# A border between two experts in a float32 MoE decoder kernel: weight split first, result read-out in pieces

## The chip, the cores and the metric

The kernel runs on one core of one Trainium2 chip. The metric is the device time of one launch in microseconds (us). Before the change it is 1759.11 us, the median of three runs (1756.7 to 1759.35). The profile is of one further execution, which took 1762.06 us.

The engines are called by these names: PE is TensorE (matrix multiplication; PEld is its weight load), DVE is VectorE, ACT is ScalarE, POOL is GpSimd, SP is SyncE, which issues the weight transfers.

## What is computed

The reference is one inference step of a small decoder trunk with two layers, for 256 prompt tokens and 8 sample tokens, all in float32. Layer 0 ends in a dense SwiGLU, layer 1 in a mixture of eight experts, of which every token uses two:

```python
def swiglu(x, wg, wu, wd):
    return (jax.nn.silu(x @ wg) * (x @ wu)) @ wd

def moe_swiglu(x, w_r, wg, wu, wd):
    logits = (x @ w_r).astype(jnp.float32)
    top_v, top_i = lax.top_k(logits, TOP_K)
    gates = jax.nn.softmax(top_v, axis=-1)
    ...
    for e in range(N_EXPERTS):
        out = out + dense_gate[..., e:e + 1].astype(x.dtype) * swiglu(x, wg[e], wu[e], wd[e])
    return out
```

The model width is 1024 and an expert's hidden width 3584. One expert's three weight matrices are 44 MB in float32.

## The kernel before, in words

The first 730 us (both mixers, the dense feed-forward, the router) are not touched. The change is in the expert stage, which runs from about 735 us to 1747 us.

**Jobs and units.** The expert stage consists of eight jobs, one for each expert. A job gathers up to 120 tokens of its expert and the 8 sample tokens into a block of 128 columns, multiplies, and adds the result back a job later. Its weights come in 42 units of 1 MB (128 partitions x 2048 values), in the order of the table STREAM (line 235): in each of 7 steps the gate weights g in two units, the up weights u in two, and from the second step on the down weights d of the step before, in two; the last two units are d of the last step. So a job begins with units 0, 1 (g), 2, 3 (u), 4, 5 (g), 6, 7 (u), 8, 9 (d), and ends with 40, 41 (d). Below, "unit 2" means unit 2 of the next job where a border between two jobs is spoken of.

**Splitting.** The products are done in the type float32r, so each unit is split in two parts whose sum is the float32 value: ACT copies the unit to w_hi (rounded), then DVE computes w_lo = unit - w_hi, and PE multiplies three times: high by high, low by high, high by low. A unit is 12 matmuls with 512 columns. There are three buffers for w_hi and three for w_lo (SPLITS = 3): the split of unit p needs PE to be through with unit p-3. The raw units lie in a ring of six (RING), which SP refills when DVE has written the w_lo of the unit six before.

**Queues.** Each engine has its own program, written out by hand in order: `job(...)` for PE at line 1348, for ACT at line 1693, for DVE at line 2278. An engine does its instructions in that order, and semaphores make one wait for another. In ACT's and DVE's programs the loop variable p runs from 3 to 44; at p the unit p is split (for p of 42 to 44 units 0 to 2 of the next job, `split(j, p)`), and the other work that goes with unit p-3 follows. PE, in its order, does the two g units, then (from step 1) the transposes of the step before, then the two u units, then down.

**Other work in a step.** When the g product is done, ACT writes silu of it (act_g, in act_place). When the u product is done, DVE multiplies it with act_g to act_h (line 2290, also in act_place). PE transposes act_h (line 1298, the operation with ident), ACT and DVE split the transpose into at_hi and at_lo, and PE multiplies that with the down weights into two banks of PSUM (Y_BANKS).

**The border.** Behind the last matmul of unit 41 the result of the job lies in the two Y banks. ACT reads each half to ysb_hi, scaled with the gate (`high_result`, line 1689). DVE's `results` (line 2256) does four operations: for each half ysb_lo = scaled bank - ysb_hi for all 128 rows, then for rows 96 to 127 (the sample tokens) acc = scaled bank + acc (shown as moe_rows). The last of them raises y_free, which PE awaits at step 1 before it writes the Y banks again. ysb_hi and ysb_lo are used by PE from step 1 of the next job (`scatter`, one quarter in each of four steps). On both engines the read-out stands ahead of `split(j, 44)`, the split of unit 2 of the next job.

ACT, DVE and PE run jobs 0 to 6 in a hardware loop and job 7 in code written out behind it. There are seven borders between jobs.

Of the kernel before, what the change touches and what calls it, by code (L numbers as in the profile page):

```python
# [23 lines left out]
F32 = mybir.dt.float32  # L24
F32R = mybir.dt.float32r
I32 = mybir.dt.int32
ALU = mybir.AluOpType
# [17 lines left out]
NE, FE = 8, 3584  # L45
# [6 lines left out]
SPLITS = 3  # L52
# [194 lines left out]
PER_JOB = len(STREAM)  # L247
# [9 lines left out]
def trunk(nc, a, o):  # L257

    with ExitStack() as ctx:
# [6 lines left out]
        bank = [ctx.enter_context(nc.psum_tensor(f"bank{i}", [P, 512], F32)) for i in range(8)]  # L266
# [165 lines left out]
        acc = carve(3, D)  # L432
# [16 lines left out]
        gslot = carve(1)  # L449
# [14 lines left out]
        ysb_hi, ysb_lo = (sb(n, [P, D], F32R) for n in ("ysb_hi", "ysb_lo"))  # L464
# [75 lines left out]
        y_free = sem("y_free")  # L540
# [859 lines left out]
        def _(act):  # L1400
# [39 lines left out]
            def split(j, p, first=False):  # L1440

                if not first:
                    used(j, p - SPLITS)
                slot = p % RING
                act.wait_ge(w_landed[slot], 16 * (landed0[slot] + j * (PER_JOB // RING) + p // RING + 1))
                f(w_hi[p % SPLITS][:, :], wring[:, slot, :]).then_inc(hi_ready, 1)
# [236 lines left out]
            def high_slots(j):  # L1683

                for i, b in enumerate(X_BANKS):
                    act.wait_ge(full[b], moe0[b] + j + 1)
                    high_part(i)
# [5 lines left out]
            def job(j, more, last=False):  # L1693


                for p in range(SPLITS, PER_JOB + SPLITS):
                    if p == PER_JOB + SPLITS - 1:
                        act.wait_ge(evac[S_BANK], moe0[S_BANK] + (j + 1) * S_FILLS)
                        if last:
                            act.wait_ge(y0_full, 1)  # L1700
                            high_result(0)
                    if p < PER_JOB:
                        split(j, p)
                    else:
                        used(j, p - SPLITS)
                    mat, s, h = STREAM[p - SPLITS]
                    n = j * STEPS + s
                    if (mat, h) == ("g", 1):
                        if s > 0:
                            act.wait_ge(full[T_BANK], moe0[T_BANK] + n)  # L1710
                            f(at_hi[:, (s - 1) % 2], bank[T_BANK][:, :]).then_inc(at_hi_ready, 1)
                        f(act_g[:, s % 2, :], bank[G_BANK][:, :], ACT.Silu).then_inc(evac[G_BANK], 1)
                    if (mat, s, h) == ("d", STEPS - 2, 1):
                        act.wait_ge(full[T_BANK], moe0[T_BANK] + n + 2)
                        f(at_hi[:, (STEPS - 1) % 2], bank[T_BANK][:, :]).then_inc(at_hi_ready, 1)
                        if not last:
                            high_slots(j)
                    if p == PER_JOB + SPLITS - 1:
                        for h in range(1 if last else 0, 2):
                            high_result(h)  # L1720
                    if p >= PER_JOB and more:
                        split(j, p)

            def last_results(n):

# [34 lines left out]
        def _(dve):  # L1760
# [21 lines left out]
            def stt(out, in0, scalar, in1, op0=ALU.mult, op1=ALU.add):  # L1782
                return V.scalar_tensor_tensor(out=out, in0=in0, scalar=scalar, in1=in1, op0=op0, op1=op1)  # L1783
# [15 lines left out]
            def split(j, p):  # L1799

                dve.wait_ge(hi_ready, j * PER_JOB + p + 1)
                tt(w_lo[p % SPLITS][:, :], wring[:, p % RING, :], w_hi[p % SPLITS][:, :].bitcast(F32), ALU.subtract
                   ).then_inc(lo_ready, 1)
# [449 lines left out]
                v = acc[:, t, 512 * h:512 * h + 512]  # L2253
                return tt(v, v, out[:, :], ALU.add)

            def results(j):

                for h in range(2):
                    dve.wait_ge(ysb_ready, 2 * j + h + 1)
                    hs = slice(512 * h, 512 * h + 512)  # L2260
                    stt(ysb_lo[:, hs], bank[Y_BANKS[h]][:, :], gslot[:, :], ysb_hi[:, hs].bitcast(F32), ALU.mult,
                        ALU.subtract).then_inc(ylo_ready, 1)
                    v = acc[ROWS[2], 2, hs]
                    ins = stt(v, bank[Y_BANKS[h]][ROWS[2], :], gslot[ROWS[2], :], v, ALU.mult, ALU.add)
                ins.then_inc(y_free, 1)

            def low_part(s, n):
                dve.wait_ge(at_hi_ready, n + 1)
# [6 lines left out]
                    dve.wait_ge(xg_hi_ready, 2 * j + 2 + i + 1)  # L2275
                    low_slots(i, bank[b]).then_inc(evac[b], 1)

            def job(j, more, last=False):

                for p in range(SPLITS, PER_JOB + SPLITS):  # L2280
                    if p < PER_JOB:
                        split(j, p)
                    mat, s, h = STREAM[p - SPLITS]
                    n = j * STEPS + s
                    if (mat, h) == ("g", 1) and s > 0:
                        low_part(s - 1, n - 1)
                    if (mat, h) == ("u", 1):
                        dve.wait_ge(evac[G_BANK], moe0[G_BANK] + n + 1)
                        dve.wait_ge(full[U_BANK], moe0[U_BANK] + n + 1)
                        tt(act_h[:, s % 2, :], act_g[:, s % 2, :], bank[U_BANK][:, :], ALU.mult  # L2290
                           ).then_inc(evac[U_BANK], 1)
                    if (mat, h) == ("d", 1) and s < 5:
                        dve.wait_ge(full[S_BANK], moe0[S_BANK] + j * S_FILLS + s + 1)
                        if s < 4:
                            add_back(bank[S_BANK], s).then_inc(evac[S_BANK], 1)
                    if (mat, s, h) == ("d", 4, 1):
                        V.tensor_copy(gslot[:, :], bank[S_BANK][:, 2 * P:2 * P + 1])
                        V.tensor_copy(sct[:, :, :], bank[S_BANK][:, 0:2 * P].rearrange("p (t n) -> p t n", t=2)
                                      ).then_inc(evac[S_BANK], 1)
                        dve.wait_ge(evac[S_BANK], moe0[S_BANK] + (j + 1) * S_FILLS)  # L2300
                        if not last:
                            choose(j + 1)
                    if (mat, s, h) == ("d", STEPS - 2, 1):
                        low_part(STEPS - 1, n + 1)
                        if not last:
                            next_low_slots(j)
                    if p == PER_JOB + SPLITS - 1:
                        results(j)
                    if p >= PER_JOB and more:
                        split(j, p)  # L2310


            for t in range(3):
# [2 lines left out]
            V.memset(sct[:, :, :].bitcast(F32), 0.0)  # L2316
            V.memset(ysb_hi[:, :].bitcast(F32), 0.0)
            V.memset(ysb_lo[:, :].bitcast(F32), 0.0).then_inc(y_free, 1)
            with dve.Fori(0, NE - 1) as j:
                job(j, True)  # L2320
            dve.wait_ge(passes_ready, 1)
            jobs = nc.values_load(passes[0:1, 0:1], engines=[DVE], min_val=NE, max_val=JOBS)
            job(NE - 1, False, last=True)
            with nc.If(jobs > NE):
                choose(NE)
                for p in range(SPLITS):
# [47 lines left out]
```

## Time and profile before

| | |
|---|---|
| Time, median of 3 runs | 1759.11 us (1756.7 to 1759.35) |
| The profiled execution | 1762.06 us |
| Its span, from the first to the last instruction | 1760.3 us |
| PE busy | 1710.1 us, 97% of the span |
| DVE busy | 1356.7 us, 77% |
| ACT busy | 1055.5 us, 60% |
| Granted TensorE clock, mean | 0.992 |
| Moved by DMA | 465.51 MB |

The span is cut from the trace of one execution. Busy shares are averages over the whole program: in the expert stage DVE and the DMA queues are far busier than in the first half. Ends of matmuls are modelled: a matmul of 512 columns is shown with about 0.39 us, but the next one starts 0.23 us after it, since they overlap. For the pace of PE the starts have to be read, not the durations. On DVE and ACT, too, an operation can start a little before the one ahead of it has ended. A wait is shown in square brackets behind the instruction that waited, with what released it.

### The profile page before, as it was taken

Reading aid. Unit: us, or ns where it says so; the run is one execution under the profiler, and the core shown is the slowest. Engines: PE = TensorE matmul, PEld = TensorE weight load, DVE = VectorE, ACT = ScalarE, POOL = GpSimd, SP = SyncE. Lnnn points to the kernel's source line nnn. Section 1 sums busy time; section 2 is a strip of 40 time slices with the busy share of each in tenths; the row PEclk is TensorE's granted clock in tenths of the full one; section 3 lists DMA queues with packets and bytes.
Section 4 is the critical chain, followed back from the end, with each engine's and each line's share of the span. In section 5 each row is a group of like instructions: output and inputs, shape, how many; then the busy total and the mean of one; then the engine's idle time right before and its main releaser. Section 6 shows DMA issues by size and latency. Waiting matters only on the chain.

```text
span 1760.3 us, 24065 instructions
## 1 busy us (share of the span) xinstructions
PE 1710.1 (97%) x8992; PEld 1440.2 (82%) x8992; DVE 1356.7 (77%) x1376; ACT 1055.5 (60%) x1013; POOL 112.3 (6%) x117
## 2 busy tenths in 40 slices
PE   7999999999999999999999999999999999999996
PEld 5877899999887789888788788788788788787885
DVE  3678766664357876688888888888888988888886
ACT  2535544433243554677777776776776766777675
POOL 2054000000105400000000000000000000000000
PEclk9999999999999999899999999999999999999999
DMA  8455354646545535499899899899899999998993
GB/s 254 144 179 180 130 173 144 187 134 180 184 132 172 189 122 190 153 362 359 316 367 354 315 363 358 322 360 351 324 358 333 346 357 322 356 360 309 368 359 111
DMA packets 257159, 465.51 MB, mean 264 GB/s; under 512 B 8492, under 2 KB 108196, under 8 KB 257056
## 3 DMA queue, kind: packets, MB, share of 16 engines
q1 hardware_dynamic: 250736, 443.28, 72.8%
q0 software_dynamic: 6064, 20.19, 3.3%
q8 instruction: 46, 0.75, 0.2%
q10 hardware_dynamic: 288, 1.08, 0.2%
q14 instruction: 25, 0.20, 0.0%
HBM read 453.70 MB, written 11.15 MB: 264 GB/s over the span
## 4 chain that ended last, share of the span: by engine, by line
PE 87%; DVE 7%; ACT 3%; issue 2%; POOL 0%; DVEq 0%; ACTq 0%; POOLq 0%
PE bank L884 84%; PE bank L888 3%; DVE arena L1783 2%; DVE w_lo L1786 1%; ACT w_hi L1414 1%; ACT arena L1414 1%; DVE moe_rows L1783 1%; DVE fw_lo L1786 1%; ACT fw_hi L1414 1%; DVE cs_t L1786 0%; DVE arena L1786 0%; DVE sam_y L1875 0%; DVE ysb_lo L1783 0%; DVE bank L1997 0%; DVE rs L1786 0%
## 5 line engine op out<-in xcount | busy, mean ns | idle before, releaser
L1786 DVE TENSOR_TENSOR w_lo<-wring,w_hi 128x2048 fp32r<-128x2048 f32 x336 | 768.4, 2291 | 109.7 <-ACT w_hi L1414 108.9
L1414 ACT ACTIVATE w_hi<-wring 128x2048 fp32r<-128x2048 f32 x336 | 644.4, 1920 | 250.4 <-PE bank L884 250.3
L884 PE MATMUL bank<-w_hi,xg_hi 128*128 128x512 f32 x896 | 357.4, 399 | 13.6 <-DVE w_lo L1786 12.1
L884 PE MATMUL bank<-w_hi,xg_lo 128*128 128x512 f32 x896 | 353.5, 395 | 0.0
L884 PE MATMUL bank<-w_lo,xg_hi 128*128 128x512 f32 x896 | 352.4, 393 | 0.0
L884 PE MATMUL bank<-hn,wring 128*128 128x264 f32 x1152 | 269.1, 391 | 8.5 <-DVE hn L1783 6.1
L884 PEld LDWEIGHTS bank<-hn,wring 128*128 128x128 f32 x1152 | 218.6, 192 | 51.5 <-issue 11.7
L884 PEld LDWEIGHTS bank<-w_hi,xg_hi 128*128 128x128 f32 x896 | 168.3, 188 | 54.7 <-DVE w_lo L1786 13.7
L884 PEld LDWEIGHTS bank<-w_lo,xg_hi 128*128 128x128 f32 x896 | 168.4, 188 | 38.1
L884 PEld LDWEIGHTS bank<-w_hi,xg_lo 128*128 128x128 f32 x896 | 168.5, 188 | 36.2
L884 PE MATMUL bank<-w_hi,at_hi 128*128 128x512 f32 x448 | 177.9, 397 | 1.8 <-DVE at_lo L1786 1.8
L1786 DVE TENSOR_TENSOR fw_lo<-wring,fw_hi 128x2048 fp32r<-128x2048 f32 (+1 forms) x54 | 113.1, 2095 | 83.7 <-ACT fw_hi L1414 83.7
L884 PE MATMUL bank<-w_lo,at_hi 128*128 128x512 f32 x448 | 176.3, 394 | 0.0
L884 PE MATMUL bank<-w_hi,at_lo 128*128 128x512 f32 x448 | 175.2, 391 | 0.0
L1414 ACT ACTIVATE fw_hi<-wring 128x2048 fp32r<-128x2048 f32 (+1 forms) x54 | 95.0, 1760 | 124.4 <-PE bank L884 124.4
L1414 ACT ACTIVATE arena<-bank 128x11 f32<-128x11 f32 (+4 forms) x96 | 31.9, 349 | 162.9 <-PE bank L884 162.9
L1783 DVE SCALAR_TENSOR_TENSOR arena<-bank,par,arena 128x255 f32<-128x255 f32 (+2 forms) x120 | 57.6, 481 | 70.8 <-ACT arena L1414 67.8
L884 PEld LDWEIGHTS bank<-w_hi,at_hi 128*128 128x128 f32 x448 | 84.1, 188 | 20.7 <-DVE at_lo L1786 2.0
L884 PEld LDWEIGHTS bank<-w_lo,at_hi 128*128 128x128 f32 x448 | 84.1, 188 | 20.2
L884 PEld LDWEIGHTS bank<-w_hi,at_lo 128*128 128x128 f32 x448 | 84.5, 189 | 19.6
L884 PE MATMUL bank<-hn_hi,fw_hi 128*128 128x264 f32 x352 | 87.6, 285 | 2.1 <-DVE xT L1786 2.1
L884 PE MATMUL bank<-hn_hi,fw_lo 128*128 128x264 f32 x352 | 87.5, 284 | 0.0
(261 smaller groups left out, 2055.4 us busy)
## 6 DMA issues: line engine op xcount, KB each, us to landing
wring<-in_moe_w_gate SPq DMA_DIRECT2D x112, 1024.0 KB, 5.7
wring<-in_moe_w_up SPq DMA_DIRECT2D x112, 1024.0 KB, 5.5
wring<-in_moe_w_down SPq DMA_DIRECT2D x112, 1024.0 KB, 5.3
wring<-in_w_in SPq DMA_DIRECT2D x36, 1024.0 KB, 5.3
wring<-in_w_out SPq DMA_DIRECT2D x16, 1024.0 KB, 5.2
wring<-in_ffn_w_gate SPq DMA_DIRECT2D x11, 1024.0 KB, 5.5
wring<-in_ffn_w_up SPq DMA_DIRECT2D x11, 1024.0 KB, 5.4
wring<-in_ffn_w_down SPq DMA_DIRECT2D x16, 704.0 KB, 4.7
```

The source lines that it names most:

```text
L884: return nc.tensor.matmul(out, lhsT, rhs, start=start, stop=stop)
L888: return nc.tensor.transpose(out, in_, ident[0:k, 0:k])
L1414: return nc.scalar.activation(out, in_, fn, **kw)
L1783: return V.scalar_tensor_tensor(out=out, in0=in0, scalar=scalar, in1=in1, op0=op0, op1=op1)
L1786: return V.tensor_tensor(out, in0, in1, op)
```

## The change

On ACT, `split(j, p)` for the last three p of a job now stands ahead of the `high_result` pair, so that at p = 44 the w_hi of unit 2 is written before ysb_hi.

On DVE, `results` is cut into `low_result` (the ysb_lo of one half) and `sample_result` (the acc rows of one half; the second raises y_free). All four are taken out of the border and put into the next job: behind the split of unit 3 stands low_result(0), behind unit 4 sample_result(0), behind unit 5 low_result(1), behind unit 6 sample_result(1), this last one ahead of act_h of step 0. Job 7 does its own four at its end, as before. Job 0 has no predecessor, so it is written out ahead of DVE's loop, which now runs jobs 1 to 6. PE's and SP's programs are unchanged.

```diff
--- before.py
+++ after.py
@@ -1715,11 +1715,11 @@
                         f(at_hi[:, (STEPS - 1) % 2], bank[T_BANK][:, :]).then_inc(at_hi_ready, 1)
                         if not last:
                             high_slots(j)
+                    if p >= PER_JOB and more:
+                        split(j, p)
                     if p == PER_JOB + SPLITS - 1:
                         for h in range(1 if last else 0, 2):
                             high_result(h)
-                    if p >= PER_JOB and more:
-                        split(j, p)
 
             def last_results(n):
 
@@ -2253,16 +2253,19 @@
                 v = acc[:, t, 512 * h:512 * h + 512]
                 return tt(v, v, out[:, :], ALU.add)
 
-            def results(j):
-
-                for h in range(2):
-                    dve.wait_ge(ysb_ready, 2 * j + h + 1)
-                    hs = slice(512 * h, 512 * h + 512)
-                    stt(ysb_lo[:, hs], bank[Y_BANKS[h]][:, :], gslot[:, :], ysb_hi[:, hs].bitcast(F32), ALU.mult,
-                        ALU.subtract).then_inc(ylo_ready, 1)
-                    v = acc[ROWS[2], 2, hs]
-                    ins = stt(v, bank[Y_BANKS[h]][ROWS[2], :], gslot[ROWS[2], :], v, ALU.mult, ALU.add)
-                ins.then_inc(y_free, 1)
+            def low_result(j, h):
+
+                dve.wait_ge(ysb_ready, 2 * j + h + 1)
+                hs = slice(512 * h, 512 * h + 512)
+                stt(ysb_lo[:, hs], bank[Y_BANKS[h]][:, :], gslot[:, :], ysb_hi[:, hs].bitcast(F32), ALU.mult,
+                    ALU.subtract).then_inc(ylo_ready, 1)
+
+            def sample_result(h):
+
+                v = acc[ROWS[2], 2, 512 * h:512 * h + 512]
+                ins = stt(v, bank[Y_BANKS[h]][ROWS[2], :], gslot[ROWS[2], :], v, ALU.mult, ALU.add)
+                if h == 1:
+                    ins.then_inc(y_free, 1)
 
             def low_part(s, n):
                 dve.wait_ge(at_hi_ready, n + 1)
@@ -2275,11 +2278,15 @@
                     dve.wait_ge(xg_hi_ready, 2 * j + 2 + i + 1)
                     low_slots(i, bank[b]).then_inc(evac[b], 1)
 
-            def job(j, more, last=False):
+            def job(j, more, results_due=False, results_later=False, last=False):
 
                 for p in range(SPLITS, PER_JOB + SPLITS):
                     if p < PER_JOB:
                         split(j, p)
+                    if results_due and p in (SPLITS, SPLITS + 2):
+                        low_result(j - 1, (p - SPLITS) // 2)
+                    if results_due and p in (SPLITS + 1, SPLITS + 3):
+                        sample_result((p - SPLITS) // 2)
                     mat, s, h = STREAM[p - SPLITS]
                     n = j * STEPS + s
                     if (mat, h) == ("g", 1) and s > 0:
@@ -2304,10 +2311,12 @@
                         low_part(STEPS - 1, n + 1)
                         if not last:
                             next_low_slots(j)
-                    if p == PER_JOB + SPLITS - 1:
-                        results(j)
                     if p >= PER_JOB and more:
                         split(j, p)
+                    if p == PER_JOB + SPLITS - 1 and not results_later:
+                        for h in range(2):
+                            low_result(j, h)
+                            sample_result(h)
 
 
             for t in range(3):
@@ -2316,11 +2325,12 @@
             V.memset(sct[:, :, :].bitcast(F32), 0.0)
             V.memset(ysb_hi[:, :].bitcast(F32), 0.0)
             V.memset(ysb_lo[:, :].bitcast(F32), 0.0).then_inc(y_free, 1)
-            with dve.Fori(0, NE - 1) as j:
-                job(j, True)
+            job(0, True, results_later=True)
+            with dve.Fori(1, NE - 1) as j:
+                job(j, True, results_due=True, results_later=True)
             dve.wait_ge(passes_ready, 1)
             jobs = nc.values_load(passes[0:1, 0:1], engines=[DVE], min_val=NE, max_val=JOBS)
-            job(NE - 1, False, last=True)
+            job(NE - 1, False, results_due=True, last=True)
             with nc.If(jobs > NE):
                 choose(NE)
                 for p in range(SPLITS):
```

DVE, the end of the loop body before (the border; w_lo here are units 0, 1 and, behind the four results, 2 of the next job):

```order
L1786 TENSOR_TENSOR w_lo<-wring,w_hi 128x2048 [waits hi_ready]
L2259 REGISTER_ALU
L1783 SCALAR_TENSOR_TENSOR ysb_lo<-bank,route,ysb_hi 128x512 [waits ysb_ready]
L1783 SCALAR_TENSOR_TENSOR moe_rows<-bank,route,moe_rows 32x512
L2259 REGISTER_ALU
L1783 SCALAR_TENSOR_TENSOR ysb_lo<-bank,route,ysb_hi 128x512 [waits ysb_ready]
L1783 SCALAR_TENSOR_TENSOR moe_rows<-bank,route,moe_rows 32x512
L1801 REGISTER_ALU
L1786 TENSOR_TENSOR w_lo<-wring,w_hi 128x2048 [waits hi_ready]
L2319 REGISTER_ALU
L2319 COMPARE_AND_BRANCH
```

In the new program the same place holds three w_lo and the branch, with nothing between them. The four results stand at the head of the loop body instead. There, before the change (w_lo are units 3 to 6, act_place is act_h of step 0):

```order
L1786 TENSOR_TENSOR w_lo<-wring,w_hi 128x2048 [waits hi_ready]
L1801 REGISTER_ALU
L1786 TENSOR_TENSOR w_lo<-wring,w_hi 128x2048 [waits hi_ready]
L1801 REGISTER_ALU
L1786 TENSOR_TENSOR w_lo<-wring,w_hi 128x2048 [waits hi_ready]
L1801 REGISTER_ALU
L1786 TENSOR_TENSOR w_lo<-wring,w_hi 128x2048 [waits hi_ready]
L2288 ISA
L1786 TENSOR_TENSOR act_place<-act_place,bank 128x512 [waits full1,evac0]
```

and the same stretch on DVE in the changed kernel, from behind unit 3's w_lo:

```order
L2258 ISA
L1783 SCALAR_TENSOR_TENSOR ysb_lo<-bank,route,ysb_hi 128x512 [waits ysb_ready]
L1801 REGISTER_ALU
L1786 TENSOR_TENSOR w_lo<-wring,w_hi 128x2048 [waits hi_ready]
L1783 SCALAR_TENSOR_TENSOR moe_rows<-bank,route,moe_rows 32x512
L1801 REGISTER_ALU
L1786 TENSOR_TENSOR w_lo<-wring,w_hi 128x2048 [waits hi_ready]
L2258 REGISTER_ALU
L1783 SCALAR_TENSOR_TENSOR ysb_lo<-bank,route,ysb_hi 128x512 [waits ysb_ready]
L1801 REGISTER_ALU
L1786 TENSOR_TENSOR w_lo<-wring,w_hi 128x2048 [waits hi_ready]
L1783 SCALAR_TENSOR_TENSOR moe_rows<-bank,route,moe_rows 32x512
```

Right behind the last of these rows comes act_h. Between unit 3's w_lo and act_h, DVE has three operations before and seven now. On ACT, the end of the loop body before and now (w_hi with w_landed0, 1, 2 are units 0, 1, 2 of the next job):

```order
L1414 ACTIVATE w_hi<-wring 128x2048 [waits w_landed1,split_used]
L1698 ISA
L1435 REGISTER_ALU [waits evac3]
L1414 ACTIVATE ysb_hi<-bank,route 128x512 [waits down_done]
L1414 ACTIVATE ysb_hi<-bank,route 128x512
L1414 ACTIVATE w_hi<-wring 128x2048 [waits w_landed2,down_done]
```

```order
L1414 ACTIVATE w_hi<-wring 128x2048 [waits w_landed1,split_used]
L1698 ISA
L1435 REGISTER_ALU [waits evac3]
L1414 ACTIVATE w_hi<-wring 128x2048 [waits w_landed2,down_done]
L1414 ACTIVATE ysb_hi<-bank,route 128x512 x2
```

Unit 2's w_hi has changed places with the two ysb_hi; all else on ACT stands where it stood.

## Rows read from the trace of the kernel before

**Rows 1.** The chain of waits, first border (start us, us, what):
```profile
857.79 0.76 DVE moe_rows L1783
...
858.58 2.30 DVE w_lo L1786
...
860.92 11.33 PE bank L884 x48
```

**Rows 2.** Waits of PE, 735 to 1745 us (total us, times, longest us):
```profile
PE bank L884 <- DVE w_lo L1786: 12.1, 8, 2.4
```

**Rows 3.** Timeline of PE, first border and step 0 of job 1 (start us, us):
```profile
853.82 0.39 PE L884 MATMUL bank<-w_hi,xg_hi 128*128 128x512 f32 x1
...
859.16 0.40 PE L884 MATMUL bank<-w_lo,xg_hi 128*128 128x512 f32 x1
860.92 0.50 PE L884 MATMUL bank<-w_hi,xg_hi 128*128 128x512 f32 x1 [1.36 <-DVE w_lo L1786]
861.26 0.39 PE L884 MATMUL bank<-w_hi,xg_lo 128*128 128x512 f32 x1
...
872.09 0.60 PE L888 MATMUL bank<-ident,act_place 128*128 128x128 f32 x4
...
878.06 0.39 PE L884 MATMUL bank<-w_hi,at_hi 128*128 128x512 f32 x1
```

**Rows 4.** Timeline of DVE, the same stretch:
```profile
853.24 2.29 DVE L1786 TENSOR_TENSOR w_lo<-wring,w_hi 128x2048 fp32r<-128x2048 f32 x1
855.45 0.75 DVE L1783 SCALAR_TENSOR_TENSOR ysb_lo<-bank,route,ysb_hi 128x512 fp32r<-128x512 f32 x1
856.23 0.76 DVE L1783 SCALAR_TENSOR_TENSOR moe_rows<-bank,route,moe_rows 32x512 f32<-32x512 f32 x1
...
857.79 0.76 DVE L1783 SCALAR_TENSOR_TENSOR moe_rows<-bank,route,moe_rows 32x512 f32<-32x512 f32 x1
858.58 6.70 DVE L1786 TENSOR_TENSOR w_lo<-wring,w_hi 128x2048 fp32r<-128x2048 f32 x3
865.93 2.29 DVE L1786 TENSOR_TENSOR w_lo<-wring,w_hi 128x2048 fp32r<-128x2048 f32 x1 [0.66 <-ACT w_hi L1414]
868.82 2.29 DVE L1786 TENSOR_TENSOR w_lo<-wring,w_hi 128x2048 fp32r<-128x2048 f32 x1 [0.59 <-ACT w_hi L1414]
871.14 0.69 DVE L1786 TENSOR_TENSOR act_place<-act_place,bank 128x512 f32<-128x512 f32 x1
```

**Rows 5.** Timeline of ACT, the same stretch:
```profile
854.01 1.27 ACT L1414 ACTIVATE ysb_hi<-bank,route 128x512 fp32r<-128x512 f32 x2 [0.81 <-PE bank L884]
855.17 1.91 ACT L1414 ACTIVATE w_hi<-wring 128x2048 fp32r<-128x2048 f32 x1
857.11 1.28 ACT L1414 ACT_TABLE_LOAD   x1
858.40 3.72 ACT L1414 ACTIVATE w_hi<-wring 128x2048 fp32r<-128x2048 f32 x2
862.14 1.28 ACT L1414 ACT_TABLE_LOAD   x1
...
863.98 1.92 ACT L1414 ACTIVATE w_hi<-wring 128x2048 fp32r<-128x2048 f32 x1
```

**Rows 6.** Timeline of DVE, job 0, unit 6's w_lo and act_h:
```profile
741.13 2.29 DVE L1786 TENSOR_TENSOR w_lo<-wring,w_hi 128x2048 fp32r<-128x2048 f32 x1 [0.79 <-ACT w_hi L1414]
743.34 0.68 DVE L1786 TENSOR_TENSOR act_place<-act_place,bank 128x512 f32<-128x512 f32 x1
```

**Rows 7.** Timeline of ACT, last border:
```profile
1620.23 1.27 ACT L1414 ACTIVATE ysb_hi<-bank,route 128x512 fp32r<-128x512 f32 x2 [0.81 <-PE bank L884]
1621.38 3.72 ACT L1414 ACTIVATE w_hi<-wring 128x2048 fp32r<-128x2048 f32 x2
```

**Rows 8.** Timeline of PE, last border:
```profile
1627.23 0.47 PE L884 MATMUL bank<-w_hi,xg_hi 128*128 128x512 f32 x1 [1.46 <-DVE w_lo L1786]
...
1638.36 0.60 PE L888 MATMUL bank<-ident,act_place 128*128 128x128 f32 x4
```

**Rows 9.** Windows, one whole job (busy us of each engine, clock, DMA share, GB/s):
```profile
981.50:1109.10 127.60, 126.23 (x581) 103.17 (x580) 111.78 (x74) 92.27 (x62) 0.00 (x0) 1.00 0.97 345
```

## The prediction, made before the changed kernel was run

> **What bounds the kernel now.** The page's busy shares come first: PE is busy 97% of the span, so what counts is what makes PE wait. The waits of PE through the whole expert stage [rows 2] show 12.1 us in 8 waits for one thing, w_lo from DVE. One of the eight is at the start of job 0 (its 2.4 us is the longest in the row); the other seven are one at each border, 1.36 us at the first [rows 3], 1.46 us at the last [rows 8]. The chain of waits [rows 1] says what is behind them: DVE's last result operation at 857.79, then w_lo at 858.58, then PE at 860.92 with 48 matmuls in a row. That w_lo is unit 2, which waits behind the four results. The windows of one whole job [rows 9] then give the room on the others: in 127.6 us DVE is busy 111.8 and ACT 92.3; the clock is 1.00; DMA is at 0.97, but the transfers that it carries are issued by w_lo six units ahead, and no wait on ACT for a landing stands in the chain. So over a job DVE has 16 us to spare. Whether it has them at the border is the question, and for that the timelines of one border are read side by side [rows 3 to 5].
>
> **What the wait costs today.** PE starts its last matmul of unit 1 at 859.16 and would start the next 0.23 us later, at 859.39. It starts at 860.92, and the first step after a wait takes 0.34 us instead of 0.23 (860.92 to 861.26) [rows 3]. So a border loses 1.53 + 0.11 = 1.64 us. From 860.92 to the transposes at 872.09 PE has four units (2 to 5) without a pause: (11.17 - 0.11) / 4 = 2.765 us a unit [rows 3].
>
> **ACT after the change.** The w_hi of unit 2 starts where ysb_hi starts now, at 854.01, released by the same matmul. It takes 1.91, so it ends at 855.93. The two ysb_hi follow and end at about 857.1. What comes then is a table load (at 857.11 now, 1.28 us), and then w_hi of units 3 and 4 from 858.40 [rows 5]. ACT does the same work in the same time, only in another order, and so unit 3's w_hi ends as it does now: 858.40 plus 0.02 for the end of the last ysb_hi, plus 1.92, at 860.34. It is not early, though unit 2's is.
>
> **DVE after the change.** Unit 1's w_lo starts at 853.24, and DVE is free again at 855.45 [rows 4]. Unit 2's w_lo starts at 855.96 behind its w_hi and ends at 858.25, 1.1 us before PE wants it at 859.39. So the wait of today goes entirely. But then DVE stands idle from about 858.2 until unit 3's w_hi arrives, at 860.37: 2.2 us, in which the four results (4 x 0.78 = 3.1 us, start to start [rows 4]) could mostly have been done. In the new order the first of them stands behind unit 3's w_lo. From 860.37 on DVE has without a break: w_lo 3, low_result(0), w_lo 4, sample_result(0), w_lo 5, low_result(1), w_lo 6, sample_result(1), act_h. A w_lo takes 2.21 us from its start to that of the next operation [rows 4, 6], a result 0.78. The sum to the start of act_h is 4 x 2.21 + 4 x 0.78 = 11.96 us. One more term: ahead of act_h a w_lo takes 2.21 in job 0 (741.13 to 743.34 [rows 6]) but 2.32 in job 1 (868.82 to 871.14 [rows 4]), where results on 32 rows came before. In the new order such operations alternate with the w_lo. I count 0.11 once, at least, and four times at most. act_h then starts at 860.37 + 12.07 = 872.44, takes 0.69, and PE is released 0.05 us later (as 860.92 stands to the end of w_lo at 860.88 [rows 1, 3]).
>
> **PE after the change.** Units: 2 at 859.39; 3 would be due at 862.16, its w_lo ends 860.37 + 2.29 = 862.66, start 862.71; 4 due at 865.59, w_lo 4 starts at 863.36 and ends at 865.65, start 865.70; 5 due at 868.58, w_lo 5 starts at 866.35 and ends at 868.64, start 868.69; the transposes due at 871.57, released at 873.18. So the one wait of 1.5 becomes three small ones (about 0.55, 0.1, 0.1) and one of 1.6 us at the transposes, which wait for act_h. Today they start at 872.09, in the new order at 873.18: **1.09 us later at each border**. Without the 0.11 it is 0.98, with it four times 1.42. Unit 6's w_lo, the wait before unit 6 and before down are covered: down of step 0 starts 5.97 us after the transposes (878.06 - 872.09 [rows 3]), at 879.15, and before it DVE has w_lo 7, w_lo 8 and at_lo, 2 x 2.21 + 0.7 from 873.05, done at 878.2. y_free, raised at about 872.4, is wanted at 879.15 too. So the delay neither grows nor is won back: PE is the bound from there on.
>
> **The last border.** There ACT has left its loop, and no table load follows: w_hi of units 2 and 3 run in one piece [rows 7]. In the new order: w_hi 2 at 1620.23, two ysb_hi of 0.58 start to start (854.01, two of them, 855.17 [rows 5]), w_hi 3 at about 1623.22, its w_lo at 1625.17, act_h 12.07 later, at 1637.24, the transposes at 1637.98. Today: 1638.36 [rows 8]. That border gains 0.38.
>
> **Other edits.** At the end of job 7 the four results stand in the same order as today: nothing. Job 0 is written out ahead of DVE's loop and the loop is entered at the first border instead of at job 0: costed at nothing, since the branch falls into DVE's 2.2 us of idle time before unit 3; without that cover its price is bounded by what DVE shows nearest, none between four w_lo that span the loop's way back (858.58, three in 6.70 us [rows 4]) below, and the 2.2 us idle above. Transfers: SP waits for w_lo; unit 2's comes 2.6 us sooner, those of 5 and 6 up to 0.5 us later, against a ring of six units (over 16 us of PE): nothing.
>
> **Sum.** 6 x 1.09 - 0.38 = +6.2 us. The profiled execution took 1762.06 us, 1.76 more than its span of 1760.30: it would be 1768.3. The median of the runs, 1759.11, is 2.95 lower, so I say 1759.1 + 6.2 = **1765.3 us**. The bounds of the 0.11 term give 6 x 0.98 - 0.49 = +5.4 and 6 x 1.42 - 0.05 = +8.5, so the forecast's own range is about 1763 to 1768.
>
> On the gap between two DVE operations the Trainium skill has two rules. The rows come first: 2.21 us from start to start for an operation of 2.29, in other places 2.32, and 0.78 for one of 0.75 [rows 4, 6]. The page "VectorE: DVE Perf Modes", section "The DRAIN you can't avoid", says that the next operation does not issue until the pipeline has emptied; by it all eight steps would be of the long kind, which is +8.5 in all, and the 2.21 speak against it. The section "Two Vector instructions with no wait between them" of the same page says that an instruction is held until its predecessors are through when its inputs or output start in another group of 32 partitions than those before; by it three of the four gaps behind a w_lo are long, and the two behind a low_result are shorter than 0.78, which by my estimate ends within 0.1 us of the sum above. That the 2.32 shows in job 1 and not in job 0 agrees with it.
>
> **Rivals.** A: DVE has the room that its 16 us a job suggest, and all seven waits simply go: -1.64 x 7 = -11.5, 1747.6 us. For it: the wait shown is the only one at a border. Against it: the transposes would have to start at 872.09 - 1.64 = 870.45, and from unit 3's w_hi at 860.37 to there are 10.1 us, with 12.8 us of DVE work in them. B, the other side: the short border of ACT's last one (no table load between ysb_hi and w_hi 3) holds for all seven, because the load at the head of ACT's loop is not met there. Its place is ACT between 857.1 and 858.4, its price 1.3 us at each border, and it decides when unit 3's w_hi ends before about 859.3 instead of 860.34: then DVE's chain ends before today's 872.09. 7 x -0.38 = -2.7, 1756.4 us. Against it: the load is of the loop's head, which the change leaves alone. C: the chain is late by less, since a result between two w_lo overlaps with them more than the 0.78 shows, which is taken from results that follow one another; at 0.55 each it would be 1.09 - 0.92 = +0.17 at six borders and -1.3 at the last, together 1758.8. Against it: the first result starts 2.21 behind a w_lo of 2.29, no closer than any other operation [rows 4]. D: the backlog does more than shift the transposes (loop entry on DVE, or w_lo 7 to 9 late as well); at a loss of twice the size, 1771.5.
>
> **Chances.** Forecast 0.62, A 0.10, B 0.06, C 0.14, D 0.08. About 0.2% (3.5 us) is what a measurement of this kernel can tell from no change. A is faster by more than that; B and C are within it; the forecast and D are slower. Faster 0.10, same 0.20, slower 0.70. The range leaves out A and the far end of D: 1756 to 1770.
>
> **What would show it.** In the changed profile PE's waits should name act_place from DVE ahead of the transposes, six times near 1.6 us and once near 1.2, and w_lo for about 0.5 us at unit 3; no wait before unit 2. DVE should be idle about 2.2 us ahead of unit 3's w_lo and then have nine operations without a gap. The time from one border to the next should grow by 1.1 us. I am wrong if the transposes come less than 0.6 us later than today after the last matmul of a job, if PE still waits for unit 2, or if a new wait appears after down of step 0.

## The result

The changed kernel takes 1762.55 us in the median of 12 runs, the kernel before 1759.23 us in 12 runs. The ratio of the two kernels, estimated from all the runs, is 1.0031, with a 95% interval of 1.0017 to 1.0045: slower, by 0.3%, or 5.5 us (3 to 8). The two medians alone differ by less, 3.3 us. The runs fall in two groups by their mean granted clock, near 0.995 and near 0.992, in which the changed kernel takes 1761.8 us (mean of 8 runs) and 1768.7 us (4) and the kernel before, in the 29 runs timed with the first experiments, 1754.7 us (12) and 1760.8 us (17): within a group the change costs 7 to 8 us, and a median depends on how many runs fall in which. The forecast was 1765.3 us, 6.2 us above 1759.1.

The two profiled executions differ by less than that: spans of 1761.4 and 1760.3 us. This is because the part ahead of the expert stage, which the change doesn't touch, is not the same length in each execution. The expert stage itself is steady: in the three traces of kernels that keep its order of work (before, and c1_peel and g4_before_act_flat below) it is 1004.53 to 1004.62 us long. So it is what the traces are compared by: from the first matmul of job 0 to the first one behind the last wait for at_lo in job 7. In the trace of before these are at 735.99 and 1740.61 (1004.62 us), in that of the changed kernel:

```profile
730.24 0.50 PE L884 MATMUL bank<-w_hi,xg_hi 128*128 128x512 f32 x1 [2.44 <-DVE w_lo L1786]
...
1741.70 0.50 PE L884 MATMUL bank<-w_hi,at_hi 128*128 128x512 f32 x1 [1.75 <-DVE at_lo L1786]
```

That is 1011.46 us: the expert stage became 6.8 us longer, where 6.2 were forecast.

### The profile page after: what moved, and what is told of

It reads as the page before. It is cut to its first block, busy times and chain, and to the rows that moved or that the text cites. A ratio compares the mean times of both kernels' runs of the same rounds, so it can differ in the third digit from the quotient of the medians.

```text
span 1761.4 us, 23994 instructions
## 1 busy us (share of the span) xinstructions
PE 1707.4 (97%) x8992; PEld 1433.3 (81%) x8992; DVE 1355.7 (77%) x1376; ACT 1055.7 (60%) x1013; POOL 112.2 (6%) x117
## 4 chain that ended last, share of the span: by engine, by line
PE 83%; DVE 10%; ACT 4%; issue 3%; DMA 0%; ACTq 0%; DVEq 0%
PE bank L884 80%; PE bank L888 3%; DVE w_lo L1786 3%; DVE arena L1783 2%; ACT w_hi L1414 1%; ACT arena L1414 1%; DVE ysb_lo L1783 1%; DVE moe_rows L1783 1%; DVE fw_lo L1786 1%; ACT fw_hi L1414 1%; ACT L1414 1%; DVE cs_t L1786 0%; ACT ysb_hi L1414 0%; DVE arena L1786 0%; DVE sam_y L1875 0%
```

## The profile after

The two largest groups of PE's waits from 700 to 1752 us (total us, times, longest us), of the changed kernel, against [rows 2]:

```profile
PE bank L888 <- DVE act_place L1786: 10.3, 7, 1.6
PE bank L884 <- DVE w_lo L1786: 5.1, 7, 2.4
```

The seven waits of 1.4 us for unit 2 are gone. In their place stand seven for act_h ahead of the transposes, 10.3 us in all. Of the 5.1 us for w_lo, 2.4 are at the start of job 0 as before, the rest are six waits of 0.45 us for unit 3. The timeline of PE at the first border, against [rows 3]:

```profile
853.45 0.40 PE L884 MATMUL bank<-w_lo,xg_hi 128*128 128x512 f32 x1
853.68 0.39 PE L884 MATMUL bank<-w_hi,xg_hi 128*128 128x512 f32 x1
...
856.20 0.39 PE L884 MATMUL bank<-w_lo,xg_hi 128*128 128x512 f32 x1
857.03 0.50 PE L884 MATMUL bank<-w_hi,xg_hi 128*128 128x512 f32 x1 [0.45 <-DVE w_lo L1786]
...
862.56 0.40 PE L884 MATMUL bank<-w_lo,xg_hi 128*128 128x512 f32 x1
862.99 0.50 PE L884 MATMUL bank<-w_hi,xg_hi 128*128 128x512 f32 x1
...
865.66 0.39 PE L884 MATMUL bank<-w_lo,xg_hi 128*128 128x512 f32 x1
867.56 0.65 PE L888 MATMUL bank<-ident,act_place 128*128 128x128 f32 x4 [1.51 <-DVE act_place L1786]
...
873.59 0.39 PE L884 MATMUL bank<-w_hi,at_hi 128*128 128x512 f32 x1
```

Unit 2 (853.68) now follows unit 1 without a gap, and unit 3 (857.03), unit 5 (862.99) and the transposes (867.56) each start late. From the last matmul of unit 1 to the transposes it takes 14.11 us, and before it took 12.93 (859.16 to 872.09): 1.18 more. From the transposes to down (873.59) it takes 6.03 us, as before the 5.97 of [rows 3]: nothing is late behind them. The timeline of DVE in the same stretch, against [rows 4]:

```profile
850.30 2.29 DVE L1786 TENSOR_TENSOR w_lo<-wring,w_hi 128x2048 fp32r<-128x2048 f32 x1 [0.48 <-ACT w_hi L1414]
854.69 2.29 DVE L1786 TENSOR_TENSOR w_lo<-wring,w_hi 128x2048 fp32r<-128x2048 f32 x1 [2.09 <-ACT w_hi L1414]
856.90 0.74 DVE L1783 SCALAR_TENSOR_TENSOR ysb_lo<-bank,route,ysb_hi 128x512 fp32r<-128x512 f32 x1
857.56 2.28 DVE L1786 TENSOR_TENSOR w_lo<-wring,w_hi 128x2048 fp32r<-128x2048 f32 x1
859.87 0.76 DVE L1783 SCALAR_TENSOR_TENSOR moe_rows<-bank,route,moe_rows 32x512 f32<-32x512 f32 x1
860.64 2.29 DVE L1786 TENSOR_TENSOR w_lo<-wring,w_hi 128x2048 fp32r<-128x2048 f32 x1
862.97 0.75 DVE L1783 SCALAR_TENSOR_TENSOR ysb_lo<-bank,route,ysb_hi 128x512 fp32r<-128x512 f32 x1
863.63 2.28 DVE L1786 TENSOR_TENSOR w_lo<-wring,w_hi 128x2048 fp32r<-128x2048 f32 x1
865.95 0.76 DVE L1783 SCALAR_TENSOR_TENSOR moe_rows<-bank,route,moe_rows 32x512 f32<-32x512 f32 x1
866.74 0.69 DVE L1786 TENSOR_TENSOR act_place<-act_place,bank 128x512 f32<-128x512 f32 x1
```

The first row is unit 2's w_lo. Behind it DVE is idle for 2.09 us and then works through nine operations without a pause, from 854.69 to act_h at 866.74: 12.05 us. What it was idle for is seen on ACT, against [rows 5]:

```profile
848.35 1.92 ACT L1414 ACTIVATE w_hi<-wring 128x2048 fp32r<-128x2048 f32 x1 [0.85 <-PE bank L884]
850.17 1.25 ACT L1414 ACTIVATE ysb_hi<-bank,route 128x512 fp32r<-128x512 f32 x2
851.44 1.28 ACT L1414 ACT_TABLE_LOAD   x1
852.73 3.73 ACT L1414 ACTIVATE w_hi<-wring 128x2048 fp32r<-128x2048 f32 x2
```

Unit 3's w_hi starts 4.38 us after unit 2's (848.35 to 852.73), as it starts 4.39 us after the first ysb_hi in [rows 5]. The chain of waits (start us, us, what) says the same in its own way. It used to enter the border through DVE's results and unit 2's w_lo [rows 1]; now it enters through ACT:

```profile
851.44 1.28 ACT L1414
...
852.73 1.93 ACT w_hi L1414
...
866.74 0.70 DVE act_place L1786
...
867.56 0.65 PE bank L888 x4
```

## The experiments

Eight kernels were run, in two groups of four. Each was timed against the kernel before, in 12 runs (e1 and g3 in 6). As the part ahead of the expert stage scatters, the table also has the length of the expert stage in the one profiled execution of each, cut as above.

| Kernel | ratio to before (95%) | expert stage us | against before |
|---|---|---|---|
| before | | 1004.62 | |
| changed | 1.0031 (1.0017 to 1.0045) | 1011.46 | +6.8 |
| c1_peel | 0.9989 (0.9972 to 1.0006) | 1004.53 | -0.1 |
| e1_act_swap | 1.0081 (1.0052 to 1.0111) | 1018.45 | +13.8 |
| e2_swap_both | 0.9993 (0.9976 to 1.0010) | 1004.56 | -0.1 |
| e3_sample_behind | 1.0014 (0.9998 to 1.0030) | 1005.54 | +0.9 |
| g1_gap_fill | 0.9967 (0.9953 to 0.9981) | 998.64 | -6.0 |
| g2_after_act_flat | 0.9997 (0.9983 to 1.0012) | 1003.79 | -0.8 |
| g3_gap_fill_act_flat | 0.9939 (0.9918 to 0.9959) | 993.13 | -11.5 |
| g4_before_act_flat | 1.0001 (0.9986 to 1.0015) | 1004.59 | 0.0 |

**c1_peel: does the written-out job 0 cost anything?**

```diff
-            with dve.Fori(0, NE - 1) as j:
+            job(0, True)
+            with dve.Fori(1, NE - 1) as j:
                 job(j, True)
```

> The kernel before, with DVE's job 0 written out ahead of its loop and nothing else changed. Theory Q (the order of DVE's work is the cause: the four results stand behind unit 3's split and push act_h): no difference, within 1 us, and PE's waits still seven of 1.36 to 1.46 us for unit 2's w_lo. Rival P (the written-out job and the entry into the loop at the first border are what costs): about 5 us slower, with a pause on DVE at the first border or a slower job 0.

Measured: 0.1 us less in the expert stage, the ratio's interval holds 1, and the seven waits at unit 2 are 1.36, 1.36, 1.37, 1.36, 1.36, 1.36 and 1.46 us. Writing out job 0 costs nothing; P falls.

**e1_act_swap: ACT's part alone.**

```diff
+                    if p >= PER_JOB and more:
+                        split(j, p)
                     if p == PER_JOB + SPLITS - 1:
                         for h in range(1 if last else 0, 2):
                             high_result(h)
-                    if p >= PER_JOB and more:
-                        split(j, p)
```

> ACT's part of the change alone: w_hi of unit 2 ahead of the two ysb_hi; DVE as before. Theory Q: DVE's first result now waits for ysb_hi(0), which ends at 856.5 in the first border's time instead of 854.7, so the four results end at 859.7 and unit 2's w_lo at 862.0; PE gets it 1.1 us later at every border: waits for unit 2 of about 2.5 us, 7 x 1.1 = 7.7 us slower. Rival R (an earlier w_hi of unit 2 helps by itself): waits at unit 2 shorter than 1.36 us, faster.

The waits came out as expected, 2.51 us at six borders and 2.60 at the last: R falls. But the time did not: +13.8 us in the expert stage, against 7.7. The longer waits make 8.0 us of it (1.14 or 1.15 at each border); the other 5.8 us go with the clock. The timeline of PE at the second border and the windows behind the first and the second (busy us of each engine, clock, DMA share, GB/s):

```profile
987.88 0.40 PE L884 MATMUL bank<-w_lo,xg_hi 128*128 128x512 f32 x1
990.78 0.79 PE L884 MATMUL bank<-w_hi,xg_hi 128*128 128x512 f32 x1 [2.51 <-DVE w_lo L1786]
...
991.80 0.63 PE L884 MATMUL bank<-w_lo,xg_hi 128*128 128x512 f32 x1
992.23 0.63 PE L884 MATMUL bank<-w_hi,xg_hi 128*128 128x512 f32 x1
...
995.18 0.39 PE L884 MATMUL bank<-w_hi,xg_hi 128*128 128x512 f32 x1
```

```profile
861.90:868.00 6.10, 6.06 (x26) 4.99 (x27) 5.47 (x3) 4.09 (x5) 0.00 (x0) 1.00 0.83 289
...
990.70:994.00 3.30, 3.22 (x8) 2.54 (x9) 3.30 (x3) 2.06 (x3) 0.00 (x0) 0.50 0.64 184
```

Behind the second border's wait the granted clock was 0.50 (1.2 GHz) for 3.3 us and the matmuls started 0.43 us apart (991.80 to 992.23) instead of 0.23; behind the first, with the same 2.51 us of wait, it was 1.00. It fell at four of the seven borders: in the 3.3 us behind the second, fourth, fifth and last wait it was 0.50, 0.53, 0.55 and 0.51, behind the other three 1.00. The four stretches that follow those (to the next border, or to the end of the stage) are longer than in the kernel before by 1.4, 1.6, 1.3 and 1.5 us more than the waits account for, and the other stretches by 0.03 us at most: together the missing 5.8 us.

**e2_swap_both: unit 2 first on both engines, the results whole.** ACT as in e1, and on DVE:

```diff
+                    if p >= PER_JOB and more:
+                        split(j, p)
                     if p == PER_JOB + SPLITS - 1:
                         results(j)
-                    if p >= PER_JOB and more:
-                        split(j, p)
```

> Unit 2 is split ahead of the results on ACT and on DVE, but the four results stay whole at the border, behind unit 2's w_lo and ahead of unit 3's. Theory Q: no wait at unit 2; the results fill DVE's idle 2.2 us and overrun it by 0.9 us, so unit 3's w_lo ends at about 863.6 where 862.2 is due: PE waits 1.4 us there, and act_h is in time. The pause only moves by one unit: within 1 us of the kernel before. Rival A (the wait at unit 2 is the only one of the border): 11.5 us faster. Rival S (ACT's late w_hi of unit 3 is what holds PE, whatever DVE does): waits of about 0.5 us at unit 3 and 6 us faster.

The waits of PE and the first of the seven:

```profile
PE bank L884 <- DVE w_lo L1786: 12.3, 8, 2.5
...
855.10 0.50 PE L884 MATMUL bank<-w_hi,xg_hi 128*128 128x512 f32 x1 [1.39 <-DVE w_lo L1786]
```

Seven waits of 1.39 to 1.40 us. The first ends 8.4 us, or three units, ahead of the transposes (which start at 863.54 in this trace), where it was 11.2 us, or four units [rows 3]: they have moved to unit 3. The expert stage is as long as before, to 0.1 us. That the wait at unit 2 goes is worth nothing as long as the results still stand ahead of unit 3's w_lo: A falls, and so does S.

**e3_sample_behind: the last piece moved behind act_h.**

```diff
-                    if results_due and p in (SPLITS + 1, SPLITS + 3):
-                        sample_result((p - SPLITS) // 2)
+                    if results_due and p == SPLITS + 1:
+                        sample_result(0)
...
                         tt(act_h[:, s % 2, :], act_g[:, s % 2, :], bank[U_BANK][:, :], ALU.mult
                            ).then_inc(evac[U_BANK], 1)
+                        if results_due and s == 0:
+                            sample_result(1)
```

> The changed kernel with only its last piece, sample_result(1), moved from ahead of act_h to behind it. Theory Q: act_h starts 0.79 us sooner at each border, so PE's wait at the transposes falls from 1.5 to 0.7 us (last border 1.2 to 0.4), 5.5 us faster than the changed kernel, which is within 2 us of the kernel before. Nothing is late at down of step 0, since y_free still comes 4 us before it. Rival P or any cause outside DVE's order ahead of act_h: as slow as the changed kernel, 5 us above before.

The waits of PE:

```profile
PE bank L884 <- DVE w_lo L1786: 5.2, 7, 2.5
PE bank L888 <- DVE act_place L1786: 4.0, 7, 0.7
```

One operation of 0.76 us, moved past one other, takes the waits at the transposes from 10.3 to 4.0 us and the expert stage from +6.8 to +0.9: 5.9 us, where 5.5 were expected. At the first border act_h comes 0.91 us sooner behind the start of unit 6's w_lo (866.39 to 868.59, against 863.63 to 866.74): the 0.79 of the piece, and 0.12 because that w_lo is followed after 2.20 us instead of 2.32. The waits fell by the same 0.9 us each. This shows that the order on DVE ahead of act_h is the cause, and that there a delay on DVE is a delay of PE, one for one. By the timed runs alone e3 can't be told from the changed kernel, since the two intervals overlap (1.0014 and 1.0031); it is the expert stage that shows it.

**g1_gap_fill: the two low_results in DVE's idle time.** On top of e3:

```diff
+                    if results_due and p == SPLITS:
+                        for i in range(2):
+                            low_result(j - 1, i)
                     if p < PER_JOB:
                         split(j, p)
-                    if results_due and p in (SPLITS, SPLITS + 2):
-                        low_result(j - 1, (p - SPLITS) // 2)
```

> The changed kernel with its four pieces at other places: both low_results at the head of the next job, ahead of unit 3's w_lo (in DVE's 2.2 us of idle time), sample_result(0) behind unit 4's w_lo as before, sample_result(1) behind act_h. Theory Q: no wait at unit 2, 0.45 us at unit 3 as in the changed kernel (ACT's w_hi of unit 3 is as late as ever), about 0.1 us at the transposes; each of the first six borders ends 0.9 us sooner than in the kernel before, the last 1.6 us: 6.8 us faster than before, 13 us faster than the changed kernel. Rival P' (moving the read-out out of the border costs wherever it lands, since DVE has no room there): waits at unit 3 or at the transposes of over 1 us, no faster than before.

The timeline of DVE at the first border:

```profile
847.91 2.29 DVE L1786 TENSOR_TENSOR w_lo<-wring,w_hi 128x2048 fp32r<-128x2048 f32 x1 [0.48 <-ACT w_hi L1414]
850.12 1.41 DVE L1783 SCALAR_TENSOR_TENSOR ysb_lo<-bank,route,ysb_hi 128x512 fp32r<-128x512 f32 x2
852.29 4.49 DVE L1786 TENSOR_TENSOR w_lo<-wring,w_hi 128x2048 fp32r<-128x2048 f32 x2 [0.77 <-ACT w_hi L1414]
856.82 0.76 DVE L1783 SCALAR_TENSOR_TENSOR moe_rows<-bank,route,moe_rows 32x512 f32<-32x512 f32 x1
```

The two results are done while DVE would have stood idle, and 0.77 us of idle time are still left. PE waits 0.44 to 0.45 us at unit 3 at six borders, and nowhere else in them. The expert stage is 6.0 us shorter than before (6.8 expected) and 12.8 shorter than the changed kernel. P' falls. Of the missing 0.8 us, 0.7 lie behind the transposes: from those of step 0 to those of step 1 it takes 17.69 us at the first six borders (mean) and 17.57 in the kernel before. What costs this 0.12 was not tried.

**g2_after_act_flat: the table load at the loop's head taken away** from the changed kernel.

```diff
-            with act.Fori(0, NE - 1) as j:
+            for j in range(NE - 1):
                 job(j, True)
```

> The changed kernel with ACT's loop over jobs 0 to 6 written out, so that the table load at the loop's head (1.28 us, between the last ysb_hi and unit 3's w_hi) goes. Theory Q: unit 3's w_hi is 1.3 us sooner at the first six borders, DVE's chain to act_h starts and ends 1.3 us sooner; no wait at unit 3, 1.3 us at the transposes, as the changed kernel has it at its last border: 8 us faster than the changed kernel, 1 to 2 us faster than before. Rival T (the chain to act_h does not start at unit 3's w_hi): as the changed kernel.

The waits of PE:

```profile
PE bank L888 <- DVE act_place L1786: 9.5, 7, 1.6
PE bank L884 <- DVE w_lo L1786: 2.5, 1, 2.5
```

The trace has no table load between 726 and 1740 us: besides the one at the loop's head, the one ahead of each job's first silu (856.48 in the changed kernel's trace, behind the w_hi of units 3 and 4) is gone too. The waits at unit 3 are gone, those at the transposes are 1.33 to 1.55 us at six borders and 1.27 at the last. The expert stage is 7.7 us shorter than the changed kernel's and 0.8 shorter than before, close to what Q says. T falls: DVE's chain does start at unit 3's w_hi. The second load has no part in it, since in the changed kernel DVE has no pause from unit 3's w_lo to act_h that ACT could shorten.

**g3_gap_fill_act_flat: both**, g1's order and ACT's loop written out (the two diffs above together).

> g1's order on DVE together with ACT's loop written out. Theory Q: no wait of PE at any border: 7 x 1.64 = 11.5 us faster than the kernel before. If a wait is left it is under 0.2 us. Rival P': not below g1.

All the waits of PE from 700 to 1752 us in it, and the DVE timeline at its first border:

```profile
PE bank L884 <- DVE w_lo L1786: 2.5, 1, 2.5
PE bank L884 <- DVE at_lo L1786: 1.7, 1, 1.7
PE bank L884 <- DVE xg_lo L1786: 1.5, 1, 1.5
PE bank L884 <- DVE ysb_lo L1783: 0.3, 1, 0.3
```

```profile
856.20 2.29 DVE L1786 TENSOR_TENSOR w_lo<-wring,w_hi 128x2048 fp32r<-128x2048 f32 x1 [0.57 <-ACT w_hi L1414]
858.40 1.40 DVE L1783 SCALAR_TENSOR_TENSOR ysb_lo<-bank,route,ysb_hi 128x512 fp32r<-128x512 f32 x2
859.72 4.48 DVE L1786 TENSOR_TENSOR w_lo<-wring,w_hi 128x2048 fp32r<-128x2048 f32 x2
864.24 0.76 DVE L1783 SCALAR_TENSOR_TENSOR moe_rows<-bank,route,moe_rows 32x512 f32<-32x512 f32 x1
```

No wait is left at any border; the four that remain are outside (ahead of job 0 and at the end of job 7). The expert stage is 11.5 us shorter than before, which is the 7 x 1.64 worked out from [rows 3]. The ratio is 0.9939 (0.9918 to 0.9959). This version is faster than both kernels.

**g4_before_act_flat: the control,** the same written-out loop on ACT in the kernel before.

> The kernel before with only ACT's loop written out (control for g2 and g3). Theory Q: unit 2's w_lo waits for DVE's results and not for ACT, so PE's wait at unit 2 stays 1.4 to 1.5 us at all borders: within 1 us of the kernel before, though ACT does 2.6 us less work a job. Rival T' (the table loads hold the border of themselves): up to 9 us faster.

```profile
PE bank L884 <- DVE w_lo L1786: 12.1, 8, 2.4
```

The same line as in [rows 2], and the same length of the stage: 2.6 us of ACT's time a job are worth nothing in the old order, and 5.5 us of the whole in g1's order (998.64 to 993.13). T' falls.

## Why the prediction was right

- **Unit 2's wait goes.** Yes, at all seven borders. e2 shows that this is worth 0 while the results stay at the border.
- **Unit 3's w_hi is as late as before, since ACT does the same work in another order.** Yes: DVE idle for 2.09 us where 2.2 was said. g2 shows it from the other side: without the table load the wait at unit 3 goes and act_h is ready sooner.
- **The chain to act_h has 12.07 us of work.** 12.05. That it came so close has two errors in it that cancel. Three of the four gaps behind a w_lo were long (2.31 to 2.33), not one; and a low_result ahead of a w_lo took 0.66 from start to start, not 0.78 (856.90 to 857.56, 862.97 to 863.63). The rule of the Trainium skill, page "VectorE: DVE Perf Modes", section "Two Vector instructions with no wait between them", gives just this pattern. The prediction set the section "The DRAIN you can't avoid" of the same page against it, but that section names the rule as its own exception, so the two aren't rivals.
- **The transposes 1.09 us late at each of six borders, 0.38 us early at the last.** From one border's transposes to the next the changed kernel takes 128.88 us (mean of five, 128.86 to 128.93), the kernel before 127.70: 1.18. The last is 127.42 against 127.79: 0.37 early. The missing 0.09 is mostly in the step from act_h to the transposes, which took 0.82 us (866.74 to 867.56), not 0.74: a small term that was sized too low.
- **Nothing late behind the transposes, nothing for the loop entry, nothing for the transfers.** The first is shown by the trace, the second by c1. (The prediction speaks of four w_lo over the loop's way back; its row has three. Nothing rests on it.) For the transfers it is only that no wait for a landing shows in the waits.
- **The sum.** +6.2 forecast, +6.8 in the expert stage of the profiled execution, +5.5 (3 to 8) by the timed runs. The median itself, 1762.55 us, is 2.8 us below the forecast 1765.3 and just under the forecast's own range of 1763 to 1768, inside that of 1756 to 1770. Eight of the 12 runs fall in the lower of the two groups, and the prediction had no term for how the runs divide.
- **Rivals.** A fell in e2: it took the one wait that shows for the only one that is near. It becomes true when DVE's results are laid where DVE is idle and ACT's load is gone (g3). B was not seen in the changed kernel, but its mechanism holds: g2 builds it, and gets -0.8 us where B said -2.7. From the first matmul of job 0 to the sixth border's transposes g2 is 0.63 us shorter than the kernel before, where B had 6 x 0.38 = 2.3, and the last border won 0.27. Its waits at the transposes are 1.33 to 1.55 us there, against 1.17 at the last border of the changed kernel; why stays open. C and D fell with the 12.05 us and with the unchanged 6.03 us to down.

## What to carry to other kernels

When an engine's queue is reordered to take away a wait, look for the next time that the same engine is awaited and add up what now stands ahead of it: a busy share of 88% over a job says nothing on the 10 us in which the engine has nearly 13 us of work. Small deferred work belongs where the engine is idle after the change, which is not where it was idle before; to know that, walk all the engines through the new order with measured start-to-start times. And an engine that feeds the bound one (here ACT) may hold the border in the new order though its load is worth nothing in the old one, so it pays to try the two edits together.

## What the hardware showed beyond that

**The clock fell behind some waits of 2.5 us, and behind none of 1.5.** In e1 the granted clock was at 0.50 to 0.55 for 3.3 us behind four of the seven waits of 2.51 to 2.60 us, and at 1.00 behind the other three. In the changed kernel, with waits of up to 1.57 us, it was 1.00 in the 3.3 us behind each of the seven. The wait of 2.43 to 2.53 us at the start of job 0 was in none of the ten traces followed by a longer first matmul (0.50 or 0.51 us). So a wait of 2.5 us may or may not cost another 1.3 to 1.6 us, and what decides it was not found. The page of a profile doesn't show such a fall: in the four slices of 44 us that hold these borders the clock of e1 stands at nine tenths or more.

**The part ahead of the expert stage scatters by more than the change is worth.** Its end (the first matmul of job 0) was at 727.4 to 736.1 us in ten profiled executions of the same code. Of the 5.75 us between the traces of the kernel before (735.99) and of the changed one (730.24), 2.9 are there at 600 us (the operation on DVE at 601.15 us in the one is at 598.29 in the other), 2.7 of them already at 31 us. The other 2.9 arise behind 712 us, where the clock differs:

```profile
710.00:720.00 10.00, 10.00 (x53) 10.00 (x53) 5.48 (x15) 4.41 (x9) 0.59 (x1) 0.54 0.15 54
```

```profile
710.00:720.00 10.00, 8.29 (x62) 7.74 (x61) 4.42 (x7) 7.39 (x12) 0.00 (x0) 0.91 0.35 108
```

The first is of the kernel before, the second of the changed one (columns as in [rows 9]); the clock is 0.54 and 0.91. Over all ten traces the end of this part goes with the clock from 700 to 720 us: at 0.76 to 0.78 (four traces) job 0 begins at 735.4 to 736.1 us, at 0.91 (two) at 730.2 and 733.0, at 1.00 (four) at 727.4 to 728.4. What sets it off was not tried. This scatter is why the spans differ by only 1.1 us, and why the experiments are read by the length of the expert stage.
